# Taking the root of a norm out of a feed-forward block's operand and multiplying it in behind the products

## The reference, cut to what matters

```python
def rmsnorm(x, g):
    y = x * lax.rsqrt(jnp.mean(x * x, axis=-1, keepdims=True) + EPS)
    return y * g
...
    x = x + m @ w_mix_out[l]                     # end of the mixer
    h = rmsnorm(x, norm2_g[l])                   # the norm "n2"
    x = x + (jax.nn.silu(h @ ffn_w1[l]) * (h @ ffn_w3[l])) @ ffn_w2[l]
    return rmsnorm(x, norm_f_g)                  # end of the first block
```

## Time and profile before

| | |
|---|---|
| median of 3 runs | 2310.08 us (2306.7 to 2312.57) |
| span of the profiled execution, first to last instruction | 2309.7 us |
| TensorE busy (matmul) | 2272.5 us, 98% |
| weight loads on TensorE | 1871.6 us, 81% |
| DVE / ACT / POOL busy | 992.4 / 898.9 / 1044.4 us |
| mean granted TensorE clock | 0.987 of full speed |

### The profile page before, as it was taken

How to read it: one execution, slowest core, us unless ns; L and a number is a source line. 1 busy time by engine, 2 the same in 40 slices (tenths; PEclk the granted TensorE clock), 3 DMA queues, 4 the chain that set the end, 5 groups by cost and what they waited for, 6 DMA issues and landing times.

```text
span 2309.7 us, 33182 instructions
## 1 busy us (share of the span) xinstructions
PE 2272.5 (98%) x10598; PEld 1871.6 (81%) x10598; DVE 992.4 (43%) x1647; ACT 898.9 (39%) x1624; POOL 1044.4 (45%) x800
## 2 busy tenths in 40 slices
PE   8999999999999999999999999999999999999997
PEld 7888888888888888888888878888677787888886
DVE  6899885526523314110014325555665555110112
ACT  4334663333322232332333354444665453332332
POOL 3455553444444443544445433333422354444444
PEclk9999999999999999999999999999999999999998
DMA  4333433337746532333333223333311432333331
GB/s 154 95 96 101 145 116 146 92 114 280 265 133 215 186 92 73 96 95 97 99 95 95 75 80 110 109 109 118 128 51 52 150 95 74 96 98 98 93 98 60
DMA packets 129483, 263.95 MB, mean 114 GB/s; under 512 B 14256, under 2 KB 14384, under 8 KB 128624
## 3 DMA queue, kind: packets, MB, share of 16 engines
q1 hardware_dynamic: 119520, 236.51, 33.7%
q10 hardware_dynamic: 9872, 26.25, 3.0%
HBM read 250.02 MB, written 12.58 MB: 114 GB/s over the span
## 4 chain that ended last, share of the span: by engine, by line
PE 89%; DVE 5%; issue 2%; ACT 2%; POOL 1%; DMA 0%; ACTq 0%; DVEq 0%; POOLq 0%
PE bank L1021 25%; PE bank L1023 25%; PE bank L1022 25%; PE bank L1290 2%; PE bank L1292 2%; PE bank L1291 2%; PE bank L1380 1%; PE bank L1343 1%; PE bank L1424 1%; POOL wlo L415 1%; PE bank L1446 1%; DVE bank L1695 1%; PE bank L1365 1%; PE bank L1193 1%; PE bank L1177 1%
## 5 line engine op out<-in xcount | busy, mean ns | idle before, releaser
L415 POOL TENSOR_TENSOR wlo<-raw,whi 128x512 fp32r<-128x512 f32 x750 | 989.3, 1326 | 1175.4 <-ACT whi L511 1174.7
L1021 PE MATMUL bank<-a_hi,whi 128*128 128x512 f32 x1928 | 762.0, 395 | 5.4 <-POOL wlo L415 2.1
L1023 PE MATMUL bank<-a_lo,whi 128*128 128x512 f32 x1928 | 751.0, 390 | 0.0
L1022 PE MATMUL bank<-a_hi,wlo 128*128 128x512 f32 x1928 | 750.3, 389 | 0.0
L511 ACT ACTIVATE whi<-raw 128x512 fp32r<-128x512 f32 x750 | 468.6, 627 | 685.0 <-PE bank L1023 612.7
L1021 PEld LDWEIGHTS bank<-a_hi,whi 128*128 128x128 f32 x1928 | 362.0, 188 | 87.2 <-issue 6.2
L1023 PEld LDWEIGHTS bank<-a_lo,whi 128*128 128x128 f32 x1928 | 361.9, 188 | 76.5
L1022 PEld LDWEIGHTS bank<-a_hi,wlo 128*128 128x128 f32 x1928 | 362.1, 188 | 75.5 <-issue 1.4
L1021 PE MATMUL bank<-b_hi,whi 128*128 128x512 f32 x852 | 336.0, 394 | 0.6 <-DVE b_lo L1833 0.3
L1023 PE MATMUL bank<-b_lo,whi 128*128 128x512 f32 x852 | 332.5, 390 | 0.0
L1022 PE MATMUL bank<-b_hi,wlo 128*128 128x512 f32 x852 | 332.5, 390 | 0.0
(11 more groups left out here) (275 smaller groups left out, 1815.8 us busy)
## 6 DMA issues: line engine op xcount, KB each, us to landing
raw<-d_stream SPq DMA_DIRECT2D x750, 256.0 KB, 2.6
G<-d_ada SPq DMA_DIRECT2D x72, 512.0 KB, 4.5
spill_rv<-tmp ACTq DMA_DIRECT2D x32, 256.0 KB, 2.1
G<-spill_rv ACTq DMA_DIRECT2D x8, 1024.0 KB, 8.2
G<-d_x ACTq DMA_DIRECT2D x4, 512.0 KB, 5.7
spill_ga<-sq ACTq DMA_DIRECT2D x8, 256.0 KB, 3.6
G<-spill_ga ACTq DMA_DIRECT2D x1, 2048.0 KB, 8.2
G<-d_x ACTq DMA_DIRECT2D x1, 2048.0 KB, 13.5
```

Source lines behind the costliest of these rows:

```text
L415: pool.tensor_tensor(wlo[:, s % SRING, :], raw[:, s % RING, :], whi[:, s % SRING, :].bitcast(F32), ALU.subtract).then_inc(lo_done, 1)
L1021: pe.matmul(out_ps, w_hi, hi[:, k, :], start=first and q == 0, stop=False)
L1022: pe.matmul(out_ps, w_lo, hi[:, k, :], start=False, stop=False)
L1023: mm = pe.matmul(out_ps, w_hi, lo[:, k, :], start=False, stop=last and q == len(ks) - 1)
```

## The change

Since silu(r·p) and r·q can be formed from the unscaled products p and q (r being the root of a token, which is a column in all tiles), the operand of `gu1a` and `gu1b` is made from X times the weight `norm2_g` alone, tile by tile, within the `mix` stage. The sums of squares and the broadcast are moved into `first_turn`, behind its k = 1 and behind its k = 2 and 3. DVE copies the broadcast row into SBUF (`ROOT_ROW`), and each pair of tiles is multiplied by it when it is taken out of the banks.

```diff
+        ROOT_ROW = sq[:, 1, :]
...
# ACT, gates_turn
+                    if name in ("gu1a", "gu1b"):
+                        done = i * 2 + (FILL_B["ffn" + name[2:]] - FILL_B["ffn1a"] + pr + 1)
+                        wait_evac(act, name, i, 2 * pr)
+                        act.activation(SIL[:, pr, :], SIL[:, pr, :], ACT.Silu).then_inc(silued, 1)
+                        wide_tick(name, i, 2 * pr + 1)
+                        act.wait_ge(gated, done)
+                        act.activation(b_hi[:, ds(i * 2 + pr, 1), :].rearrange("p a t -> p (a t)"), tmp[:, pr, :],
+                                       ACT.Copy).then_inc(b_hi_w, 1)
+                        continue
...
# ACT, mix
                 wait_evac(act, "mix", 0, m)
+                act.activation(a_hi[:, m, :], X[:, m, :], ACT.Copy, scale=col("norm2_g", m)).then_inc(a_hi_w, 1)
                 square(NORM["n2"], m, X[:, m, :])
-            round_a("hf1", 16, name="gu1a")
+            tick("gu1a", 0, 0, 4)
...
# TensorE, first_turn (behind the panels of k == 1, and behind those of k = 2 and 3)
+                    if beside and k == 1:
+                        beside[0]()
...
+                if beside:
+                    beside[1]()
                 wide_turn(name, 0, ops, ready, fill, (1,))
...
-                            first_turn(name, OPA, opa, fill)
+                            first_turn(name, OPA, opa, fill, (lambda: sum_up(NORM["n2"]), lambda: broadcast(4)))
...
-            sum_up(NORM["n2"])
-            broadcast(4, warm=5)
-            keep_warm(10)
             ffn(1, NORM["nf"], True, FILL_A["hf1"])
...
# DVE
+            def scaled_pair(name, i, pr, at):
+                done = i * 2 + (at - FILL_B["ffn1a"] + pr + 1)
+                wait_used(dve, name, i, 4 + 2 * pr)
+                dve.tensor_tensor(SIL[:, pr, :], bank_of(name, 2 * pr)[:, :], ROOT_ROW, ALU.mult)\
+                   .then_inc(evac_of(name, 2 * pr), 1)
+                wait_used(dve, name, i, 5 + 2 * pr)
+                dve.wait_ge(opb, i * 2 + (at + pr - 1))
+                dve.tensor_tensor(tmp[:, pr, :], bank_of(name, 2 * pr + 1)[:, :], ROOT_ROW, ALU.mult)\
+                   .then_inc(evac_of(name, 2 * pr + 1), 1)
+                dve.wait_ge(silued, done)
+                wait_evac(dve, name, i, 2 * pr + 1)
+                dve.tensor_tensor(tmp[:, pr, :], SIL[:, pr, :], tmp[:, pr, :], ALU.mult).then_inc(gated, 1)
+                dve.wait_ge(b_hi_w, i * 2 + (at + pr + 1))
...
+            def unscaled_lo(k):
+                dve.wait_ge(a_hi_w, FILL_A["hf1"] + k + 1)
+                wait_evac(dve, "mix", 0, k)
+                dve.scalar_tensor_tensor(out=a_lo[:, k, :], in0=X[:, k, :], scalar=col("norm2_g", k),
+                                         in1=a_hi[:, k, :].bitcast(F32), op0=ALU.mult, op1=ALU.subtract).then_inc(opa, 1)
             for m in range(KD):
                 wait_used(dve, "mix", 0, 2 * m + 1)
                 dve.tensor_tensor(X[:, m, :], X[:, m, :], bank_of("mix", m)[:, :], ALU.add)\
                    .then_inc(evac_of("mix", m), 1)
+                if m:
+                    unscaled_lo(m - 1)
+            unscaled_lo(KD - 1)
             norm_stat(NORM["n2"])
-            operand_a("hf1", lambda k: col("norm2_g", k))
+            own.next(dve.tensor_copy(ROOT_ROW, BCAST[:, :]))
             ffn(1, True)
```

More of the change, by code:

```diff
@@ L256, in build @@
         sq_ready = sem("sq_ready")
+        silued, gated = sem("silued"), sem("gated")
         sq_summed = sem("sq_summed")
@@ L771, in _ @@
                 wait_evac(act, "mix", 0, m)
+                act.activation(a_hi[:, m, :], X[:, m, :], ACT.Copy, scale=col("norm2_g", m)).then_inc(a_hi_w, 1)
                 square(NORM["n2"], m, X[:, m, :])
-            round_a("hf1", 16, name="gu1a")
+            tick("gu1a", 0, 0, 4)
             ffn(1, NORM["nf"])
-            round_a("hf2", 24, lambda k: mods[:, k:k + 1], "gu2a")
+            round_a("hf2", 16, lambda k: mods[:, k:k + 1], "gu2a")
             ffn(2, NORM["post1"])
-            round_a("hmix2", 32, lambda k: mods[:, 24 + k:25 + k], "qka")
+            round_a("hmix2", 24, lambda k: mods[:, 24 + k:25 + k], "qka")
             for t in range(8):
@@ L999, in _ @@
                 weighted_square(1, m)
-            round_a("hf3", 40, lambda k: mods[:, 48 + k:49 + k], "gu3a")
+            round_a("hf3", 32, lambda k: mods[:, 48 + k:49 + k], "gu3a")
             ffn(3, NORM["post3"])
@@ L1534, in ada_block @@
                 dve.wait_ge(ada_used, i * 8 + (8 * mod0 + s + 1 + ADA_SLOTS))
+            def scaled_pair(name, i, pr, at):
[11 more added lines that the diff above has]
+                dve.wait_ge(b_hi_w, i * 2 + (at + pr + 1))
+                dve.tensor_tensor(b_lo[:, ds(i * 2 + pr, 1), :].rearrange("p a t -> p (a t)"), tmp[:, pr, :],
+                                  b_hi[:, ds(i * 2 + pr, 1), :].rearrange("p a t -> p (a t)").bitcast(F32),
+                                  ALU.subtract).then_inc(opb, 1)
             def gate_pair(name, i, pr, at):
+                if name in ("gu1a", "gu1b"):
+                    scaled_pair(name, i, pr, at)
+                    return
                 wait_evac(dve, name, i, 2 * pr)
@@ L1840, in _ @@
                    .then_inc(evac_of("mix", m), 1)
+                if m:
+                    unscaled_lo(m - 1)
+            unscaled_lo(KD - 1)
+            filled["a"] = FILL_A["hf1"] + KD
             norm_stat(NORM["n2"])
-            operand_a("hf1", lambda k: col("norm2_g", k))
+            own.next(dve.tensor_copy(ROOT_ROW, BCAST[:, :]))
             ffn(1, True)
```

## The result

The changed kernel takes 2313.95 us (median of 12 runs, 2310.2 to 2314.98), the kernel before 2309.69 (12 runs): ratio 1.0019, 95% interval 1.0012 to 1.0027. The change costs 4.3 us, where I had forecast 1.6 us less.

A forecast was written before the change was run, and what follows sets the result against it. TensorE, busy 98% of the span, was taken as the bound. 9.5 - 1.7 - 1.1 - 2.0 - 2.4 - 0.7 = 1.6 us less gave 2308.5 us, range 2303 to 2315.5.

The forecast's parts named there:

- Later turns: no cost: Turns with modulation after the first: panel 10 has 1.8 us to spare, the last pair 1.6 us, so nothing is lost.
- What the change takes away: TensorE between `mix` and `gu1a`, 8.97 us, plus the old wait for panel 9, 0.5 us: 9.5 us less.
- What it adds on TensorE: Column sums and broadcast now standing among products: 1.7 + 1.1 = 2.8 us more; the root itself costs nothing.
- A first wait, panel 3: Start of `gu1a`: TensorE waits about 2.0 us for panel 3, split by ACT behind the last square.
- A second wait, panel 8: First turn of `gu1a`: TensorE waits 2.4 us for panel 8, behind DVE's modulation blocks and first pair.
- A third, panel 10: First turn of `gu1a`: TensorE waits 0.7 us for panel 10, as DVE empties bank 2 late.
- Rival 2, the clock: TensorE's granted clock falls behind the panel waits, costing 1.7 to 3.4 us: 2310.2 to 2311.9; chance 0.28 with rival 4.
- rival 4: The new chain changes nothing: the waits eat the whole gain, 2310 us; chance 0.28 together with Rival 2, the clock.
- the sign that I had set: On TensorE, a clock that falls in a wait would show the forecast wrong; no size given.
- Rival 3, the pair chain passes its slack: DVE's pair chain, held by POOL, exceeds 1.8 us slack every turn, costing 7 to 19 us: 2315.5 to 2327; chance 0.12.
- A rule weighed: DVE and POOL both reading SBUF: disturbance costs 0.7 us on DVE, 0.3 on POOL, rather than the skill's whole-instruction exclusion.

The follow-up runs named there:

- experiment 1: Changed kernel with ACT making panel 3's high part ahead of the high part and square of the last `mix` tile: 2311.35 us, ratio 1.0008 to the kernel before.
- experiment 6: Changed kernel with DVE's order in gu1a's first turn changed (three blocks, pair, three, pair, two) and ACT's split ahead of Silu: 2307.74 us, ratio 0.9991.
- experiment 3: Changed kernel with matmuls that nobody reads put into TensorE's waits for panels 3 and 8 and the last modulation sums: 2311.19 us, ratio 1.0009.
- experiment 4: Changed kernel with sums, root and broadcast put back ahead of the feed-forward block, unscaled operand and scaled pairs kept: 2312.6 us, ratio 1.0017.
- experiment 2: Changed kernel with each half's last modulation sum moved later, behind the second product's first panel or the next turn's panel 2: 2308.29 us, ratio 0.9996.
- experiment 7: Changed kernel with panel 3's split first, last modulation sums later and first turn reordered, all together: 2299.38 us (6 runs), ratio 0.9964 to the kernel before.

## Why the prediction was wrong, point by point

The waits for panels 3 and 8 came, within 0.2 us. Two steps failed. "Later turns: no cost" left out the sums of the last modulation vector, which cost 2.4 us; with them the sum of the prediction turns from 1.6 us less to 0.8 more. And the sum had nothing for the granted clock, which I kept as a rival because the waits have dense products on both sides; the falls cost a net 4.1 of the 4.7 us that the profile shows.

- **What the change takes away**: 8.97 us were there to take and were taken, and the old wait for panel 9 went too. Right.
- **What it adds on TensorE**: 1.7 + 1.1 us forecast. The broadcast moved panel 4 by 0.94 us; from the start of k = 1 to that of k = 2 the changed kernel loses 3.28 us, sums and a fall of the clock, and experiment 1, without the fall, 1.72. Right.
- **A first wait, panel 3**: 2.0 forecast, 1.97 measured, and experiment 1 shows that it is ACT's order. Right.
- **A second wait, panel 8**: 2.4 forecast, 2.23 and 2.46 measured; experiment 6 takes it away by the order of the first turn. Right.
- **A third, panel 10**: 0.7 forecast, not there in the changed kernel, where the half clock from 532 slowed TensorE and so covered it. In experiments 1, 3 and 4, where the clock held there, it is there, 0.59, 0.60 and 0.60 us; experiment 1 has three waits for panels (the others are panel 3's 0.63 and panel 8's 2.02):

```profile
PE bank L1035 <- POOL wlo L417: 3.2, 3, 2.0
```

  The term was right, and hidden by another.
- **Later turns: no cost.** This step failed. Turn for turn it was right: from panel 10 to the last product of `gu1a` the shift of the changed kernel doesn't move (in experiment 2 it moves 0.6, behind the wait at 561.71). But I followed only the panels and the second product, not the modulation's own consumer. TensorE sums the last modulation vector directly behind the last turn. In the kernel before that sum started on time, right behind the last product, with DVE's last block over at 650.97:

```profile
649.69 1.28 DVE L1531 SCALAR_TENSOR_TENSOR G<-G,small,bank 128x1024 f32<-128x1024 f32 x1
...
650.85 0.39 PE L1023 MATMUL bank<-a_lo,whi 128*128 128x512 f32 x1
651.08 1.89 PE L1193 MATMUL bank<-ones,G 128*128 128x1 f32 x16
```

  DVE's last block in a turn is the second of the two between the pairs; in the changed kernel it stands behind two more products of the first pair, of which the one of the linear part comes after TensorE has finished the bank and so delays all behind it by 0.7 us; and the pair product took 1.58 us (below). The block ended at 652.3:

```profile
646.38 1.58 DVE L1562 TENSOR_TENSOR tmp<-G,tmp 128x512 f32<-128x512 f32 x1
648.88 0.69 DVE L1564 TENSOR_TENSOR b_lo<-tmp,b_hi 128x512 f32 x1 [0.92 <-ACT b_hi L576]
...
649.68 1.29 DVE L1544 SCALAR_TENSOR_TENSOR bank<-G,small,bank 128x1024 f32<-128x1024 f32 x1
651.00 1.28 DVE L1544 SCALAR_TENSOR_TENSOR G<-G,small,bank 128x1024 f32<-128x1024 f32 x1
```

  In the turns within the loop the same sum waits three panels and costs nothing. The two last ones cost 1.60 us (from the last product of `gu1a` to the first of the second product) and 0.83 (around 790) in the first profile, 2.4 together; in the second 0.81 and 1.24.
- **Rival 2, the clock**: I gave it a chance of 0.28 with rival 4 and priced one fall, 1.7 to 3.4 us. There were three in each profile, of 1.6 us each (1.60 at 505, 1.61 at 532 once the old wait of 0.57 is counted back, 1.64 at 655), 4.9 us together. This step failed too: my argument against it, dense products on both sides of the wait, was wrong, and the sign that I had set, that the clock falls in a wait, came. This was the larger part: without the falls the change would have come out near 0: -8.97 + 2.01 + 1.70 + 0.94 + 2.23 - 0.57 + 1.60 + 0.83 = -0.2. To that comes 0.8, since the half clock at 532 had hidden the wait for panel 10: where the clock held, from panel 8 to the last product the shift goes up by 0.3 (experiments 1 and 3) and not down by 0.6. That makes +0.6, and +4.73 is in the table, so the falls cost a net 4.1; in the timed runs 4.3 is measured for the whole change.
- **Rival 3, the pair chain passes its slack**: out. DVE's pair product took 0.69 in 20 of 22 pairs, 1.30 and 1.58 in the other two. In both of these a POOL operation was already running when it began:

```profile
598.63 1.29 POOL L417 TENSOR_TENSOR wlo<-raw,whi 128x512 fp32r<-128x512 f32 x1 [3.73 <-ACT whi L513]
599.17 1.30 DVE L1562 TENSOR_TENSOR tmp<-G,tmp 128x512 f32<-128x512 f32 x1
...
646.12 1.29 POOL L417 TENSOR_TENSOR wlo<-raw,whi 128x512 fp32r<-128x512 f32 x1 [4.01 <-ACT whi L513]
```

  By the Trainium skill ("SBUF — State Buffer", section "SBUF: two separate sides") the later of the two is held until the other is through. The trace agrees: POOL's two operations ended at 599.92 and 647.41, DVE's at 600.47 and 647.96, 0.55 us behind each. In 14 other pairs POOL began during the pair product; then DVE kept its 0.69, and POOL ended 1.14 to 1.17 us behind DVE.
- **A rule weighed**: my reading, that the two disturb each other for 0.7 us on DVE and 0.3 on POOL, was wrong. In this trace every one of the 21 DVE operations with two SBUF inputs (pair products, `b_lo`, `a_lo`) that began with over 0.2 us of a POOL operation left ended 0.545 to 0.550 us behind POOL's end, whether it took 0.76 or 1.78. The 1.36 us at 518.50 was such a case too, with 0.81 us of POOL left. It cost little here because the order of the program lets DVE begin second so seldom in the pair product; but it came in the turn whose last sum was waited for longest (1.39 us, against 0.59 at the same place in the second profile).

## What to carry to other kernels

When work is moved off a stage that waits, look at what that stage's length had been covering: a weight panel split late, a side computation begun late, a last sum that had a tenth of a microsecond to spare. Follow every consumer of the delayed engine to the end of its loop, since the last pass has no next turn to hide in. And price a wait of a microsecond or more on TensorE with the half clock that can follow it: where products stood behind the wait it cost 1.6 us more, nearly as much as the wait.

## What the runs showed of the hardware

- A wait of 2.0 to 2.7 us between dense products was followed by 3.4 us at half clock in six of eight cases: behind panel 3's wait in both profiles of the changed kernel and in experiment 6, not in experiment 2; behind panel 8's in both of the changed kernel and in experiment 2, not in experiment 1. The same program had its falls at other waits in two executions. Waits of 0.5 to 0.65 us without column sums beside them were followed by none: panel 10's in experiments 1, 3 and 4 (both profiles), panel 3's in 1 and 7. Ahead of the modulation sums four of five waits of 1.0 to 1.4 us were followed by one, and two of eight of 0.4 to 0.7. In the one execution with the waits filled with matmuls, three were not followed by a fall; the fourth, with 0.4 us left ahead of the modulation sums, was.
- A DVE operation with two SBUF inputs and POOL's `wlo` run one after the other, as above: the one that begins second ends a fixed time behind the first, 0.54 to 0.56 us for DVE (over 0.2 us of POOL left) and 1.13 to 1.18 for POOL, in all ten profiles. So `b_lo`, which begins with 0.2 us of POOL left in most turns, has a median of 0.77 in the changed kernel.
